# Feed-forward of a hybrid recurrent decoder step: PSUM banks for the main sums, 2 to 3, and for lifted weights, 3 to 2

## The chip, the cores and the metric

The kernel runs on one core of a Trainium2 chip. The metric is the device time of one execution in microseconds (us). Matrix products run on TensorE (PE in the profile; its weight loads are PEld), elementwise work on VectorE (DVE), ScalarE (ACT) and GpSimd (POOL), and SyncE (SP) issues most of the loads. PSUM has 8 banks of 512 fp32 values in each of its 128 partitions; products end there.

## The reference, cut to what matters

One inference step over 512 prompt tokens and 64 sample tokens (576 columns here), width 1024, two layers. Each layer has a SwiGLU feed-forward before its mixer and one behind it, so there are four of them, all with the same shapes (hidden width 2816):

```
def swiglu(x, w_in, w_out):
    a, b = jnp.split(x @ w_in, 2, axis=-1)
    return (jax.nn.silu(a) * b) @ w_out
...
        x = x + 0.5 * swiglu(rmsnorm(x, norm_ffn1[i]), ffn1_w_in[i], ffn1_w_out[i])
...
        x = x + 0.5 * swiglu(rmsnorm(x, norm_ffn2[i]), ffn2_w_in[i], ffn2_w_out[i])
```

## The kernel before, in words

Every product of two fp32 matrices is made of three matmuls of a shorter float type: each operand is split into a high part (a rounded copy) and a low part (what the rounding left), and high x high, low x high and high x low are added up in PSUM.

The greater part of each feed-forward is a list of 30 **units** (`ffn_units`). Units 0 to 2, 7 to 12, 17 to 22 and 27 to 29 are "in" units (one hidden tile of 128 each: its columns of `w_in`), units 3 to 6, 13 to 16 and 23 to 26 are "out" units (two output tiles of x each, over one third of the first 18 hidden tiles). A unit multiplies with a scheme of seven products on blocks of half size, numbered q = 1 to 7, instead of eight; for that the weights are added and subtracted in pairs first (on POOL, `weight_sum`, L2454), and so are the inputs. An "in" product is 12 matmuls of 288 columns, an "out" product 9, all issued at L944 in `pair_product`.

The order of the products is written out by hand (`PE_ORDER`, L87). In step c of the list TensorE issues (c,1), (c-1,7), (c,5), (c,6), (c-1,4), (c-1,3), (c,2), where (u,q) is product q of unit u; the last two of a unit that ends a third (`closes`: units 1, 11, 21, 29) change places. Every other engine has its own order of the same list, and each is a strict queue.

PSUM in this part of the kernel: products 1, 6, 7 and 4 of a unit add up in one bank, the **main sum** (`WBANK`); 5 and 3 in another (`ZBANK`); 2 in bank 3 (`XBANK`). While the sum grows, other engines take it out between the products: after product 1 (semaphore `out1`: a copy on ACT for an "in" unit, an addition to x on DVE, `add_half`, L1796, for an "out" unit), after 6, after 7, and at the end after 4 (`out4`: `last_of_sums` on DVE, L1824 for an "in" unit, L1796 for an "out" unit). Banks change with the unit's number, so the first product of a unit waits until the unit that last had its bank is done: `first_products`, L958, waits for `out4`; product 5 waits for `out3` of the unit two before; product 6 waits for `out1` of its own unit.

**Lifted weights.** For each of the 7 weight blocks of a unit the high part is made on ACT or POOL (`high`), and ACT also copies the fp32 block into a PSUM bank (`lift`, L1228), from where DVE reads it to make the low part (`low`, L1787, a subtraction that writes `wl` or `ff_more_low`). The lifts have one order, `LIFT_ORDER` (L98), and take the banks of a ring in turn; lift number n waits until `low` has read what lay in its bank.

**Hidden blocks.** The hidden tiles come in pairs; DVE and ACT turn a pair into the blocks that the "out" units multiply with (`hidden_sums`, L1880 to L1886; `blocks_high` on ACT, L1277; `blocks_low` on DVE, L1865; semaphore `hb_low`). The last pair of a third is made while the first "out" unit behind it is already in step: its product 1 waits for the first of four blocks of each pair, 5 for two of them, 6 for all four (`blocks_ready`, L949). In DVE's queue the order around an "out" unit that follows a third is: `third_sum`, `low` (4), `last_of_sums`, the gating, `hidden_sums` of the last pair, `low` (6), `first_sum` and `low` (3) of the unit before, `blocks_low` of the last pair (twice), then `add_half` of the out unit's product 1.

On POOL, `high` (L2430) of a weight block waits until the unit before has used the same buffer on TensorE (`product_done`).

Of the kernel before, what the change touches and what calls it, by code (L numbers as in the profile page):

```python
# [52 lines left out]
def ffn_units(f, n):  # L53

    units = []

    def put(kind, **at):
        units.append(Unit(kind, N_UNITS * f + len(units), n + HEAD + 2 * len(units), **at))

    j = HEAD // 2  # L60
    for part in range(3):
        while j <= PART * (part + 1):
            put("in", j=j)
            j += 1
        for m in range(NB // 2):
            put("out", part=part, m=m)
    while j < NTILE:
        put("in", j=j)
        j += 1
    return units  # L70


N_UNITS = NTILE - HEAD // 2 + 3 * NB // 2


def in_order(steps):


    at = {}
    for c in range(-1, N_UNITS + 1):  # L80
        for back, q in steps:
            if 0 <= c - back < N_UNITS:
                at[c - back, q] = len(at) + 1
    return at
# [13 lines left out]
LIFT_ORDER = in_order(((1, 3), (0, 2), (-1, 1), (0, 7), (-1, 5), (0, 4), (-1, 6)))  # L98
# [3 lines left out]
LIFTED = {at: key for key, at in LIFT_ORDER.items()}  # L102
# [60 lines left out]
def count(name, n):  # L163

    n = n if isinstance(n, Lin) else Lin(n)
    assert n.lowest() >= 0 and (not n.k or n.lowest() > 0 or name in FROM_ONE), name
    return (n + 1 if name in FROM_ONE else n).value()
# [7 lines left out]
def build(nc, d, out):  # L175

    at = [16512]
# [9 lines left out]
    ps = nc.alloc_psum_tensor("ps", [P, 8, 512], F32)  # L187
# [57 lines left out]
    def slot(unit, q, low):  # L245
        first = unit.n % 2
        if q in (1, 5, 6):
            return more[low][:, (1, 5, 6).index(q), :]
        ring = (wh, wl)[low][:, first if q in (2, 7) else 1 - first, :]
        return ring[:, 0:512] if q in (2, 3) else ring[:, 512:1024]  # L250

    WBANK, ZBANK, XBANK = (4, 5), (6, 7), 3

    def lift_slot(w, q):
        return ps[:, LIFT_ORDER[w.v % N_UNITS, q] % 3, :]

    def bank(unit, q):
        b = XBANK if q == 2 else (ZBANK if q in (3, 5) else WBANK)[unit.v % 2]
        return ps[:, b, 0:TH]

    at[0] = free
# [73 lines left out]
    def S(name):  # L335
        if name not in sems:
            sems[name] = nc.alloc_semaphore(name)
        return sems[name]
# [12 lines left out]
    for layer in range(2):  # L351
        for kind in ("ffn", "ab" if layer == 0 else "ret", "ffn", "ple"):
            phases.append(dict(kind=kind, layer=layer, n=n, u=u, norm=norm, j=ffj))
            if kind == "ffn":
                units = ffn_units(ffj // TAIL, n)
# [25 lines left out]
    def past(eng, name, n):  # L381

        if n > 0:
            eng.wait_ge(S(name), n)
# [8 lines left out]
    def lo_ready(eng, w, q):  # L393

        if q in (3, 4):
            eng.wait_ge(S("lo_made"), w.n + (2 if q == 3 else 1))
        else:
            eng.wait_ge(S("w_low"), reached(SPLIT_ORDER, w, q))
# [134 lines left out]
    def _(pe):  # L533
# [50 lines left out]
        def gated_group(ns, n, u, i, pair, previous_norm, following=True):  # L584
# [4 lines left out]
            def scores(lev):  # L589
# [25 lines left out]
                for s in range(ns):  # L615
                    j = lev * ns + s
                    bank = 4 + j % 2
                    if j >= 2:
                        pe.wait_ge(S("picked"), count("picked", G("picked", j - 1)))
                    else:  # L620
                        pe.wait_ge(S("orms"), count("orms", G("orms", 0)))
                    for c in range(CH):
                        t = slice(c * P, (c + 1) * P)
                        last = nc.tensor.matmul(ps[:, bank, t], lhsT=ka[rows[s], t], rhs=qa[rows[s], t],
                                                start=True, stop=True)
                    if ns == 1 and lev <= 3:
                        if j:
                            pe.wait_ge(S("picked"), count("picked", G("picked", j)))
                        last = sample(s)
                    last.then_inc(S("scores"), 1)  # L630
# [301 lines left out]
        def pair_product(w, q, free, reached, ready=None):  # L932


            past(pe, free, reached)
            lo_ready(pe, w, q)
            blocks = xt if w.kind == "in" else None
            for k in range(w.pairs):
                if ready is not None:
                    pe.wait_ge(S(ready[0]), ready[1](k))  # L940
                t = slice(k * P, k * P + P)
                for wt, r in ((0, 0), (0, 1), (1, 0)):
                    rhs = (blocks[r][:, k, BLOCK[q], :] if blocks else hblocks[r][k][:, BLOCK[q], :])
                    last = nc.tensor.matmul(bank(w, q), lhsT=slot(w, q, wt)[:, t], rhs=rhs,  # L944
                                            start=(k == 0 and (wt, r) == (0, 0) and q in (1, 5, 2)),
                                            stop=(k == w.pairs - 1 and (wt, r) == (1, 0)), skip_group_check=True)
            last.then_inc(S("product"), 1)

        def blocks_ready(w, units, t):  # L949

            f = w.v // N_UNITS
            if w is units[0]:
                return "xt_low", lambda k: 2 * KP * f + 2 * k + min(t, 2)
            if w.kind == "out" and w.m == 0:
                return "hb_low", lambda k: 4 * 9 * f + 4 * (PART // 2 * w.part + k) + t
            return None

        def first_products(w, units):  # L958

            pair_product(w, 1, "out4", w.v - 1, blocks_ready(w, units, 1))  # L960

        def second_products(w, units):

# [14 lines left out]
        for ph_ in phases:  # L978
            n, u, norm = Lin(ph_["n"]), Lin(ph_["u"]), ph_["norm"]
            if ph_["kind"] == "ffn":  # L980
                j0, units = ph_["j"], ph_["units"]
# [76 lines left out]
    def _(act):  # L1058
# [129 lines left out]
        def ffn(norm, n, u, j0, units):  # L1188
# [14 lines left out]
            def source(w, q):  # L1203

                if q == 1:
                    half_landed(act, w, "11")
                    return half(w.n, 0)
                if q == 2:
                    half_landed(act, w, "12")
                    return half(w.n, 1)  # L1210
                if q == 4:
                    half_landed(act, w, "2")
                    return half(w.n + 1, 1)
                act.wait_ge(S("sum"), reached(SUM_ORDER, w, {7: 3, 5: 1, 6: 2, 3: 4}[q]))
                return half(w.n + 1, 0) if q == 7 else wsum[:, {5: 0, 6: 1, 3: 2}[q], :]

            def lift(w, q):

                c = slice(0, w.pairs * P)
                src = source(w, q)  # L1220
                at = LIFT_ORDER[w.v % N_UNITS, q]
                k, q_before = LIFTED[at - 3]
                lo_ready(act, units[k], q_before)
                if at <= 6:
                    for b in range(2):
                        act.wait_ge(S(f"taken{(u + b).mod(2)}"),
                                    count(f"taken{(u + b).mod(2)}", (u + (HEAD + b)).div(2)))
                nc.scalar.activation(lift_slot(w, q)[:, c], src[:, c], ACT.Copy)\  # L1228
                    .then_inc(S("hi_made" if q in (3, 4) else "lifted"), 1)
# [11 lines left out]
            def snapshot(w, dst, q, free, reached):  # L1241

                past(act, free, reached)
                product_done(act, w, q)
                nc.scalar.activation(dst, bank(w, q), ACT.Copy).then_inc(S(f"out{q}"), 1)
# [39 lines left out]
            w = units[0]  # L1285
# [19 lines left out]
            for c in range(N_UNITS + 1):  # L1305
# [8 lines left out]
                if old:  # L1314
                    lift(old, 3)
# [7 lines left out]
                if new:  # L1323
                    high(new, 2)
                    lift(new, 2)
                if ahead:
                    high(ahead, 1)
                    lift(ahead, 1)
# [217 lines left out]
    def _(dve):  # L1546
# [191 lines left out]
        def ffn(norm, n, u, j0, units):  # L1738
# [33 lines left out]
            def low(w, q):  # L1772

                c = slice(0, w.pairs * P)
                if q in (1, 2):
                    dve.wait_ge(S("act_high"), reached(ACT_HIGH_ORDER, w, q))
                else:
                    dve.wait_ge(S("pool_high"), reached(POOL_HIGH_ORDER, w, q))
                if w is units[0] and q in (1, 5, 6):
                    src = {1: half(w.n, 0), 5: wsum[:, 0, :], 6: wsum[:, 1, :]}[q]  # L1780
                else:
                    src = lift_slot(w, q)
                    if q in (3, 4):
                        dve.wait_ge(S("hi_made"), w.n + (2 if q == 3 else 1))
                    else:
                        dve.wait_ge(S("lifted"), reached(SPLIT_ORDER, w, q) - 3 * (f + 1))
                nc.vector.tensor_tensor(slot(w, q, 1)[:, c], src[:, c], slot(w, q, 0)[:, c], ALU.subtract)\  # L1787
                    .then_inc(S("lo_made" if q in (3, 4) else "w_low"), 1)
# [980 lines left out]
```

## Time and profile before

| | us |
|---|---|
| median of 3 runs | 3002.8 (2998.47 to 3004.94) |
| the profiled execution, its own time | 2996.45 |
| its span, first to last instruction | 2994.8 |
| outside the span | 1.65 |
| TensorE busy in the span | 2715.7 (91%) |
| VectorE busy | 1975.1 (66%) |
| ScalarE busy | 1253.6 (42%) |
| GpSimd busy | 1434.6 (48%) |

The unit lists of the four feed-forwards begin at 73.9, 937.5, 1430.3 and 2546.2 us of the span. A busy TensorE is matmuls in the pipe, not matmuls at full speed: each row carries the granted clock beside it where it matters (1.00 is 2.4 GHz, 0.50 is 1.2 GHz). In a timeline the bracket behind an instruction is the idle time of its engine just before it and what ended that time.

### The profile page before, as it was taken

To read this page: it belongs to the slowest core of one execution; us is meant where nothing else is said; L and a number is where in the kernel's file an instruction comes from. 1 tells how busy PE (TensorE), PEld (TensorE's weight loads), DVE (VectorE), ACT (ScalarE), POOL (GpSimd) and SP (SyncE) were. 2 spreads that over 40 slices of the span, in tenths; PEclk is the share of its full clock that TensorE was granted. 3 is DMA by queue.
4 is the path that set the end of the run, shared out by engine and by line. 5 is a ranking of instruction groups with operands and counts; after the bars stand their busy time and mean duration, and the time that the engine had idled before them with its cause. 6 is when DMAs were issued, how large, how long until landed. Compare 5 with 4: busy or idle time off the path is not lost. (4 is left out here: it accounts for less than half of the span.)

```text
span 2994.8 us, 51957 instructions
## 1 busy us (share of the span) xinstructions
PE 2715.7 (91%) x19034; PEld 2566.9 (86%) x19034; DVE 1975.1 (66%) x2876; ACT 1253.6 (42%) x2267; POOL 1434.6 (48%) x1469
## 2 busy tenths in 40 slices
PE   7899999899888999998899999889897979899997
PEld 7899998788788999998899998687786869899996
DVE  7887767765658788648877854352625247877865
ACT  4565553222134556534565552122122224565552
POOL 4677734443227777515677742130303116677731
PEclk9999999999989999999999999989998989999998
DMA  3223221121122222321223223412323222222221
GB/s 121 82 81 97 88 96 65 56 72 53 37 63 69 94 87 81 98 91 57 75 93 91 82 85 105 155 61 106 111 84 138 78 99 74 79 84 94 88 87 60
DMA packets 109059, 255.92 MB, mean 85 GB/s; under 512 B 12496, under 2 KB 37216, under 8 KB 108816
## 3 DMA queue, kind: packets, MB, share of 16 engines
q1 hardware_dynamic: 96192, 206.73, 21.5%
q0 software_dynamic: 12624, 45.98, 4.2%
q8 instruction: 150, 2.46, 0.3%
q14 instruction: 93, 0.76, 0.1%
HBM read 227.88 MB, written 24.77 MB: 84 GB/s over the span
## 5 line engine op out<-in xcount | busy, mean ns | idle before, releaser
L1787 DVE TENSOR_TENSOR wl<-ps,wh 128x512 fp32r<-128x512 f32 (+1 forms) x480 | 304.2, 634 | 172.5 <-ACT ps L1228 100.9
L1552 DVE TENSOR_TENSOR wl<-raw,wh 128x1024 fp32r<-128x1024 f32 x169 | 224.7, 1330 | 219.8 <-ACT wh L1066 218.9
L944 PE MATMUL ps<-ff_x_high,wh 128*128 128x288 f32 x1152 | 345.9, 300 | 0.0
L944 PE MATMUL ps<-ff_x_low,wh 128*128 128x288 f32 x1152 | 345.9, 300 | 0.0
L944 PE MATMUL ps<-ff_x_high,wl 128*128 128x288 f32 x1152 | 344.5, 299 | 0.0
L562 PE MATMUL ps<-xh,wh 128*128 128x288 f32 x1248 | 301.4, 324 | 32.6 <-DVE xl L1574 19.0
L1228 ACT ACTIVATE ps<-ff_w_sums 128x512 f32<-128x512 f32 (+1 forms) x352 | 190.7, 551 | 309.4 <-POOL ff_w_sums L2454 309.2
L1066 ACT ACTIVATE wh<-raw 128x1024 fp32r<-128x1024 f32 x169 | 178.0, 1054 | 319.6 <-PE ps L540 191.4
L944 PE MATMUL ps<-ff_x_high,ff_more_high 128*128 128x288 f32 x864 | 257.4, 298 | 30.0 <-DVE ff_hidden L1824 26.1
L562 PEld LDWEIGHTS ps<-xh,wh 128*128 128x128 f32 x1248 | 207.7, 197 | 80.8 <-issue 59.3
L562 PE MATMUL ps<-xh,wl 128*128 128x288 f32 x1248 | 274.8, 303 | 0.0
L562 PE MATMUL ps<-xl,wh 128*128 128x288 f32 x1248 | 273.9, 302 | 0.0
L1787 DVE TENSOR_TENSOR ff_more_low<-ps,ff_more_high 128x512 fp32r<-128x512 f32 (+1 forms) x348 | 218.9, 629 | 71.9 <-POOL ff_more_high L2430 47.9
L1228 ACT ACTIVATE ps<-raw 128x512 f32<-128x512 f32 (+1 forms) x476 | 256.6, 545 | 11.5 <-DVE ff_more_low L1787 11.5
L944 PE MATMUL ps<-ff_x_low,ff_more_high 128*128 128x288 f32 x864 | 255.8, 296 | 0.0
L944 PE MATMUL ps<-ff_x_high,ff_more_low 128*128 128x288 f32 x864 | 255.6, 296 | 0.0
L2430 POOL CAST wh<-raw 128x512 fp32r<-128x512 f32 (+1 forms) x240 | 149.0, 621 | 191.2 <-PE ps L944 185.8
L2454 POOL TENSOR_TENSOR ff_w_sums<-raw,ff_w_sums 128x512 f32<-128x512 f32 (+1 forms) x120 | 157.0, 1308 | 162.1 <-issue 129.8
L944 PEld LDWEIGHTS ps<-ff_x_high,wh 128*128 128x128 f32 x1152 | 223.3, 194 | 0.0
L944 PEld LDWEIGHTS ps<-ff_x_low,wh 128*128 128x128 f32 x1152 | 223.2, 194 | 0.0
L944 PEld LDWEIGHTS ps<-ff_x_high,wl 128*128 128x128 f32 x1152 | 222.6, 193 | 0.0
L562 PEld LDWEIGHTS ps<-xl,wh 128*128 128x128 f32 x1248 | 208.0, 196 | 0.0
(339 smaller groups left out, 7549.9 us busy)
## 6 DMA issues: line engine op xcount, KB each, us to landing
raw<-in_w SPq DMA_DIRECT2D x169, 512.0 KB, 3.4
raw<-in_w SPq DMA_DIRECT2D x288, 256.0 KB, 2.6
raw<-in_w SPq DMA_DIRECT2D x192, 192.0 KB, 2.3
rS<-in_s_ret POOLq DMA_DIRECT2D x32, 512.0 KB, 6.2
out_ret_s<-rS POOLq DMA_DIRECT2D x32, 512.0 KB, 3.7
x<-in_xT SPq DMA_DIRECT2D x8, 288.0 KB, 5.9
out_yT<-x SPq DMA_DIRECT2D x8, 288.0 KB, 2.2
S<-in_s_hgrn POOLq DMA_DIRECT2D x4, 512.0 KB, 3.6
```

The costliest lines, as they stand in the source:

```text
L562: last = nc.tensor.matmul(ps[:, 2 * s + a, 0:TH], lhsT=wt[:, slot, w], rhs=rhs(r, k)[:, a * TH:(a + 1) * TH], start=(k == 0 and j == 0), s ...
L944: last = nc.tensor.matmul(bank(w, q), lhsT=slot(w, q, wt)[:, t], rhs=rhs, start=(k == 0 and (wt, r) == (0, 0) and q in (1, 5, 2)), stop=(k ...
L1066: nc.scalar.activation(wh[:, n.mod(2), :], raw[:, r, :], ACT.Copy).then_inc(S("hi_made"), 1)
L1228: nc.scalar.activation(lift_slot(w, q)[:, c], src[:, c], ACT.Copy)\
L1552: nc.vector.tensor_tensor(wl[:, n.mod(2), :], raw[:, n.mod(NRAW), :], wh[:, n.mod(2), :], ALU.subtract)\
L1787: nc.vector.tensor_tensor(slot(w, q, 1)[:, c], src[:, c], slot(w, q, 0)[:, c], ALU.subtract)\
L2430: nc.gpsimd.tensor_copy(slot(w, q, 0)[:, c], src[:, c]).then_inc(S("pool_high"), 1)
L2454: nc.gpsimd.tensor_tensor(out_[:, c], in0[:, c], in1[:, c], op).then_inc(S("sum"), 1)
```

## The change

The main sums get three banks in turn (4, 5, 2) in place of two, and the first product of a unit waits for the unit three before it in place of two before. Bank 2 is taken from the ring of lifted weights: it has two banks (0, 1) in place of three, and a lift waits for the `low` two before it in the order in place of three before. No instruction is added or removed, and none changes its place in its engine's queue.

```diff
-    WBANK, ZBANK, XBANK = (4, 5), (6, 7), 3
+    WBANK, ZBANK, XBANK = (4, 5, 2), (6, 7), 3
 
     def lift_slot(w, q):
-        return ps[:, LIFT_ORDER[w.v % N_UNITS, q] % 3, :]
+        return ps[:, LIFT_ORDER[w.v % N_UNITS, q] % 2, :]
 
     def bank(unit, q):
-        b = XBANK if q == 2 else (ZBANK if q in (3, 5) else WBANK)[unit.v % 2]
+        b = XBANK if q == 2 else ZBANK[unit.v % 2] if q in (3, 5) else WBANK[(unit.v + 1) % 3]
         return ps[:, b, 0:TH]
...
         def first_products(w, units):
 
-            pair_product(w, 1, "out4", w.v - 1, blocks_ready(w, units, 1))
+            pair_product(w, 1, "out4", w.v - 2, blocks_ready(w, units, 1))
...
                 at = LIFT_ORDER[w.v % N_UNITS, q]
-                k, q_before = LIFTED[at - 3]
+                k, q_before = LIFTED[at - 2]
                 lo_ready(act, units[k], q_before)
```

## Rows read from the trace of the kernel before

**Rows 1.** Waits of TensorE, whole span: total us, times, longest us.

```profile
PE ps L944 <- DVE ff_hidden L1824: 47.6, 32, 5.4
PE ps L944 <- DVE x L1796: 33.0, 10, 3.9
```

**Rows 2.** Timeline of TensorE, first feed-forward, stops: start us, us, instruction.

```profile
94.38 0.40 PE L944 MATMUL ps<-ff_x_high,ff_more_high 128*128 128x288 f32 x1 [2.71 <-DVE ff_hidden L1824]
...
111.18 0.85 PE L944 MATMUL ps<-ff_blocks_a,ff_more_high 128*128 128x288 f32 x2 [5.40 <-DVE ff_hidden L1824]
...
182.37 0.40 PE L944 MATMUL ps<-ff_x_high,ff_more_high 128*128 128x288 f32 x1 [1.46 <-DVE ff_hidden L1824]
...
194.13 0.40 PE L944 MATMUL ps<-ff_x_high,ff_more_high 128*128 128x288 f32 x1 [0.37 <-DVE ff_hidden L1824]
...
216.96 0.53 PE L944 MATMUL ps<-ff_blocks_a,ff_more_high 128*128 128x288 f32 x2 [0.31 <-DVE ff_hidden L1824]
...
225.10 0.53 PE L944 MATMUL ps<-ff_blocks_a,ff_more_high 128*128 128x288 f32 x2 [3.90 <-DVE x L1796]
```

**Rows 3.** Timeline of VectorE and TensorE, first feed-forward, steps 3 and 4.

```profile
106.23 0.77 DVE L1865 TENSOR_TENSOR ff_blocks_b<-ff_hidden,ff_blocks_b 128x288 fp32r<-128x288 f32 x1
...
115.54 1.88 DVE L1865 TENSOR_TENSOR ff_blocks_b<-ff_hidden_sums,ff_blocks_b 128x864 fp32r<-128x864 f32 x1
117.34 0.44 DVE L1796 SCALAR_TENSOR_TENSOR x<-ps,x 128x288 f32<-128x288 f32 x1
...
117.84 0.53 PE L944 MATMUL ps<-ff_blocks_a,ff_more_high 128*128 128x288 f32 x2
```

**Rows 4.** All waits of VectorE between 99 and 117.7 us.

```profile
DVE wl L1787 <- ACT ps L1228: 1.8, 2, 1.1
```

**Rows 5.** Windows (columns: PE, PEld, DVE, ACT, POOL busy; PEclk, DMA): first, third feed-forward.

```profile
111.18:117.84 6.66, 6.66 (x30) 6.43 (x30) 5.91 (x11) 4.50 (x9) 2.53 (x3) 0.59 0.19 60
...
1468.29:1474.96 6.67, 5.75 (x30) 5.51 (x31) 5.92 (x11) 4.50 (x9) 2.75 (x3) 0.74 0.18 59
```

**Rows 6.** Windows of 9 us behind a restart of TensorE, same columns.

```profile
117.84:126.84 9.00, 9.00 (x69) 9.00 (x69) 7.67 (x18) 4.35 (x10) 6.46 (x10) 1.00 0.29 87
...
1950.84:1959.84 9.00, 9.00 (x45) 8.43 (x46) 6.83 (x6) 2.09 (x4) 5.57 (x4) 0.69 0.16 58
...
225.10:234.10 9.00, 9.00 (x56) 9.00 (x57) 6.16 (x14) 3.39 (x8) 4.93 (x8) 0.81 0.26 70
...
1582.31:1591.31 9.00, 9.00 (x49) 9.00 (x50) 5.48 (x12) 2.80 (x7) 4.82 (x7) 0.70 0.22 66
```

**Rows 7.** Timeline of TensorE: the stop ahead of the second of those windows.

```profile
1950.84 0.82 PE L884 MATMUL ps<-sqsum,ones 128*128 128x288 f32 x1 [7.82 <-POOL sqsum L2545]
```

**Rows 8.** Timeline of VectorE: `low` (2,2), first and third feed-forward.

```profile
98.20 0.69 DVE L1787 TENSOR_TENSOR wl<-ps,wh 128x512 fp32r<-128x512 f32 x1 [0.78 <-ACT ps L1228]
...
1456.45 0.69 DVE L1787 TENSOR_TENSOR wl<-ps,wh 128x512 fp32r<-128x512 f32 x1 [2.17 <-ACT ps L1228]
```

**Rows 9.** All waits of VectorE between 182 and 224.9 us.

```profile
DVE wl L1787 <- ACT ps L1228: 2.7, 4, 0.8
DVE wl L1787 <- POOL wh L2430: 2.0, 2, 1.6
```

**Rows 10.** Timeline of GpSimd and VectorE, first feed-forward, steps 12 and 13.

```profile
215.20 0.62 POOL L2430 CAST wh<-raw 128x512 fp32r<-128x512 f32 x1 [2.43 <-PE ps L944]
...
215.85 0.69 DVE L1787 TENSOR_TENSOR wl<-ps,wh 128x512 fp32r<-128x512 f32 x1 [1.56 <-POOL wh L2430]
```

**Rows 11.** Timeline of ScalarE and VectorE: lift (2,5), `low` (2,1), `low` (2,5).

```profile
89.49 0.59 ACT L1228 ACTIVATE ps<-ff_w_sums 128x512 f32<-128x512 f32 x1
...
92.09 0.68 DVE L1787 TENSOR_TENSOR ff_more_low<-ps,ff_more_high 128x512 fp32r<-128x512 f32 x1
...
93.28 0.68 DVE L1787 TENSOR_TENSOR ff_more_low<-ps,ff_more_high 128x512 fp32r<-128x512 f32 x1
```

## The prediction

> **What bounds the kernel now.** I read the table of waits first. Inside the unit lists TensorE stops for two reasons only: 47.6 us in 32 stops for L1824, the last sum of an "in" unit, and 33.0 us in 10 stops for L1796, an addition to x [rows 1]. The first is the wait that the change loosens: a unit's first product wants the bank of the unit two before. The second looks like the same wait and is not. The timeline of the first feed-forward [rows 2] shows the stops in order: 2.71 (unit 2), 5.40 (unit 3, the first "out" unit), then 1.46, 0.37 and 0.31 ahead of units 10, 11 and 13, and 3.90 at 225.10. That last one is not at the first product of a unit: it is product 6 of unit 13, 8.1 us later, and what it waits for is `out1` of its own unit, the addition of product 1 to x. A third bank for main sums does not touch it. Units 20, 21, 23 repeat the pattern, so a feed-forward has 8 stops for L1824, and 4 x 8 = 32.
>
> So the question is what else holds TensorE where the stops are. Both stretches with stops lie around the end of a third, where VectorE makes the blocks of the last hidden pair on top of its sums and low parts, and VectorE is late there by its own queue. Between 99 and 117.7 us it waits 1.8 us in all, for ScalarE and never for TensorE [rows 4]. TensorE's product (3,6) needs the addition that VectorE ends at 117.34 + 0.44 = 117.78, and starts at 117.84 [rows 3]. That it is bound by VectorE the windows show best: from the start of (3,1) to the start of (3,6) it takes 6.66 us in the first feed-forward and 6.67 in the third, though TensorE ran at a granted clock of 0.59 in the one and of 0.74, with 0.9 us of idle, in the other [rows 5].
>
> **The change part by part.** Nothing is added, removed or moved in a queue, so no operation, load or issue has a new price. What changes is two waits: `out4` gets a whole step more room, the lifts lose one bank of room. No DMA hangs on either: the loads of weights wait for low parts and sums of units that keep their place.
>
> (a) Units 2 and 3, the first two stops of each feed-forward (8.11 us in the first). Without them the first block that (3,1) still waits for is written by 106.23 + 0.77 = 107.0 [rows 3]; from there 3 matmuls of (3,1), 12 of (2,7) and 9 of (3,5), at 9.00 / 69 = 0.13 us each [rows 6], bring TensorE to (3,6) at 107.0 + 3.1 = 110.1. There it waits for the addition at 117.78 as before: one stop of 7.7 us in place of the two. VectorE's chain up to that addition has no wait for TensorE that could shrink [rows 4], so the gain is 0 (bounds: 0, and 5.40 if the chain came along). In the third feed-forward there is one: `low` (2,2) waited 2.17 us there and 0.78 in the first [rows 8], because the late (2,1) held up ScalarE's copy ahead of it. I take 1.2 us of gain, once (bounds 0 and 1.4).
>
> (b) The clock. Before, TensorE leaves (3,6) at full clock: 69 matmuls in 9 us, granted clock 1.00; it had gone slow after the stop of 5.40 and came back while it would have waited anyway. With one stop of 7.7 us right ahead of (3,6) it restarts slow. The nearest row is the restart after a stop of 7.82 us [rows 7]: clock 0.69 over the next 9 us, which is 9 x 0.31 = 2.8 us of lost work; after a stop of 3.90 it is 0.81, so 1.7 [rows 6]. I take the middle, 2.2, four times: 8.8 us slower (bounds 0 and 4 x 2.8 = 11.2). The Trainium skill, "TensorE: Matmul & The Clock Gate", section "What's actually happening", puts it as "the default state is throttled, and activity releases the throttle". The trace agrees, with 0.69 behind the longest stop; by that rule, gathering two stops into a longer one is a loss by itself.
>
> (c) Units 10, 11, 13 and 20, 21, 23: stops of 1.46 + 0.37 + 0.31 = 2.14 us, eight times. TensorE comes earlier to (13,6) and waits there for VectorE. What survives is what VectorE's chain gains. From 182 to 224.9 us it waits 2.7 us for ScalarE, which itself follows VectorE's sums, and 2.0 us in two waits for GpSimd [rows 9]; the larger, 1.56 us, is `low` (12,4) behind a cast that GpSimd could not start before TensorE's product (11,4) had ended [rows 10]. Only these 2.0 come back when TensorE is earlier. I take half, 0.95, since the lift of the same block on ScalarE ends soon after: 8 x 0.95 = 7.6 us faster (bounds 0 and 2.0 each). The stop at (13,6) grows from 3.90 to 3.90 + 2.14 - 0.95, about 5.1. After the 3.90 the clock over 9 us was 0.81 in one case and 0.70 in another [rows 6], so the longer stop costs between 0 and 9 x 0.11 = 1.0 more; I take 0.3, near the smaller as the stop is nearer to 3.90 than to 7.82: 2.4 us slower.
>
> (d) The ring of two. A lift now waits for the `low` two before. The worst place that I found is lift (2,5): it started at 89.49, ahead of the time, and would have to wait for `low` (2,1) to end, 92.09 + 0.68 = 92.77; with 0.59 for itself it is done at 93.36, while `low` (2,5) started at 93.28 [rows 11]. With the signals between, some 0.3 us late, inside VectorE's late chain: 4 x 0.3 = 1.2 us slower. Elsewhere the early lifts lie far ahead of their use and the wait costs nothing; if that cover is gone, a lift is late by up to the whole 92.77 - 89.49 = 3.3 us. Behind a waiting lift stand ScalarE's snapshots and SiLUs, which VectorE's sums release anyway. Bounds: 0 and 4 x 3.3 = 13.2.
>
> Sum: -1.2 (a) + 8.8 (b) - 7.6 + 2.4 (c) + 1.2 (d) = +3.6 us. On the profiled execution's own 2996.45 that is 3000; the median of the runs, 3002.8, lies 6.35 above that execution, and by it the forecast is **3006 us**. About 0.2%, 6 us, is what a measurement can tell from no change, so this is no change with a lean to slower.
>
> **The rivals.** *The stops simply go.* The stops for L1824 vanish and nothing late stands behind them: 3002.8 - 47.6 = 2955. The Trainium skill, "Perfetto Trace Analysis", section "Identifying Performance Opportunities", says that the same gap repeating on the engine that should be saturated can mean too few buffers; by that rule the third bank is the cure. The trace does not bear it out: (3,6) keeps its time whatever TensorE did [rows 5]. *VectorE comes along.* The wait for GpSimd goes whole and no restart is slower than now: 8 x 2.0 = 16 us faster, 2987. For it: 2.0 us in [rows 9] hang on TensorE. Against it: ScalarE's lift. *The clock decides.* The place is the restart at (3,6), and at (13,6) and (23,6): where a stop has grown, the slow clock lasts as in the worst rows, 4 x 2.8 + 8 x 1.0 = 19.2 us, and VectorE gains nothing: 3022, slower. It decides if the stops at (3,6) are 7 us and more. *The ring of two holds VectorE back*: 13.2 us, 3016; it shows as longer waits of L1787 for L1228 (1.8 and 2.7 us in the two stretches now [rows 4, 9]). That the change doesn't do what it says has no room: the counts of `out4` and the banks agree.
>
> **How the numbers follow.** The forecast gets 0.50, and its own range is 2997 to 3012: 0.42 of it within 0.2%, 0.06 above, 0.02 below. The stops go: 0.06. VectorE comes along: 0.13. The clock decides: 0.21. The ring: 0.10, of which 0.02 within. Faster 0.02 + 0.06 + 0.13 = 0.21; same 0.42 + 0.02 = 0.44; slower 0.06 + 0.21 + 0.08 = 0.35. The range reaches from just below VectorE coming along to just under the clock's full price, 2984 to 3020; it leaves out the 0.06 at 2955 and the ends.
>
> **What would show it.** In the profile of the changed kernel no stop of L944 for L1824 is left; the stops for L1796 rise from 33.0 us in 10 to some 4 x 7.7 + 8 x 5.1 = 72 us in 12; (3,6) starts within 0.5 us of where it did against the list's begin, save in the third feed-forward; the 9 us behind it read a clock below 0.9. If (3,6) starts 3 us or more earlier, (a) is wrong and with it the forecast; if the clock behind it is 1.00, (b) is; if L1787's waits for L1228 double, (d) is too small.

## The result and the profile after

The changed kernel takes 3003.2 us, the median of 20 runs (2999.7 to 3009.2), against 2998.0 us (2991.7 to 3004.9) in 20 runs of the kernel before on the same chip: a ratio of 1.0018, with a 95% interval of 1.0012 to 1.0025. That is 5 us slower: less than the 0.2% (6 us) below which the prediction speaks of no change, though the interval keeps clear of 1. The profiled execution took 3008.81 us (span 3006.9, mean granted clock 0.956, before 0.961); it lies 5.6 us above its median and the one of before 1.6 us below its own, so the two traces differ by 12.4 us where the medians differ by 5.2. The unit lists now begin at 72.7, 943.0, 1439.6 and 2556.2 us.

TensorE's waits in the changed kernel (total us, times, longest us), to be read against [rows 1]:

```profile
PE ps L944 <- DVE x L1796: 61.8, 12, 7.3
...
PE ps L944 <- issue: 11.5, 7, 2.8
...
PE ps L944 <- DVE ff_more_low L1787: 5.8, 4, 2.0
...
PE ps L944 <- DVE ff_c L1815: 3.7, 8, 0.5
PE ps L944 <- DVE ff_a L1834: 2.5, 8, 0.4
```

All 32 stops for L1824 are gone, 47.6 us of them. The stops for an addition to x have grown by 28.8 us, and there are 12 of them, one at product 6 of each first output unit of a third. The rest came back in small stops: the last three rows are new, and the second had

```profile
PE ps L944 <- issue: 3.9, 4, 1.0
```

before. With a last stop of 0.2 us, all that TensorE waits in the unit lists (L944) is 84.5 us before and 85.5 after: the bank moved its idle time and took none of it away. The timeline of TensorE, first feed-forward, shows where ([rows 2] before; start us, us, instruction, idle before it):

```profile
105.76 0.57 PE L944 MATMUL ps<-ff_blocks_a,ff_more_high 128*128 128x288 f32 x1 [2.79 <-issue]
...
116.95 0.61 PE L944 MATMUL ps<-ff_blocks_a,ff_more_high 128*128 128x288 f32 x1 [5.45 <-DVE x L1796]
...
125.24 0.43 PE L944 MATMUL ps<-ff_blocks_a,ff_more_high 128*128 128x288 f32 x2
...
226.04 0.61 PE L944 MATMUL ps<-ff_blocks_a,ff_more_high 128*128 128x288 f32 x1 [4.72 <-DVE x L1796]
```

Product (3,1) starts at 105.76, 33.0 us into the list in place of 37.2 (111.18 before). Product (3,6) starts 44.2 us into it in place of 43.9, so the 4.2 us won at (3,1) are waited away again: 5.45 us at one product. The line at 125.24 is (4,1); the kernel before had it at

```profile
123.51 0.43 PE L944 MATMUL ps<-ff_blocks_a,ff_more_high 128*128 128x288 f32 x2
```

From (3,6) to (4,1) are 5.67 us there (117.84 to 123.51) and 8.29 us here, with the same work. The four windows of 9 us behind (3,6) say why (columns: busy us and instructions of PE, PEld, DVE, ACT, POOL; the granted clock; DMA share and GB/s):

```profile
116.95:125.95 9.00, 9.00 (x48) 9.00 (x49) 5.39 (x12) 3.19 (x8) 4.81 (x7) 0.67 0.20 66
987.36:996.36 9.00, 9.00 (x48) 9.00 (x49) 5.45 (x12) 3.11 (x8) 4.52 (x7) 0.67 0.23 66
1484.39:1493.39 9.00, 9.00 (x55) 9.00 (x56) 6.09 (x14) 3.80 (x9) 4.84 (x7) 0.79 0.26 67
2600.53:2609.53 9.00, 9.00 (x55) 9.00 (x56) 6.07 (x14) 3.78 (x9) 4.86 (x7) 0.79 0.23 67
```

Before, the clock behind this product was 1.00 in all four feed-forwards [rows 6 for the first]. Now 0.33, 0.33, 0.21 and 0.21 of 9 us are missing: 9.7 us of full clock. The same windows behind product 6 of units 13 and 23, after:

```profile
226.04:235.04 9.00, 9.00 (x47) 9.00 (x48) 5.38 (x12) 3.13 (x7) 4.82 (x7) 0.67 0.21 66
335.17:344.17 9.00, 9.00 (x47) 9.00 (x48) 5.33 (x12) 3.08 (x7) 4.82 (x7) 0.66 0.21 67
1096.46:1105.46 9.00, 9.00 (x47) 9.00 (x48) 5.39 (x12) 3.14 (x7) 4.82 (x7) 0.67 0.23 66
1205.60:1214.60 9.00, 9.00 (x47) 9.00 (x48) 5.34 (x12) 3.10 (x7) 4.82 (x7) 0.66 0.22 66
1592.60:1601.60 9.00, 9.00 (x51) 9.00 (x52) 5.61 (x13) 3.59 (x8) 4.87 (x7) 0.73 0.23 66
1701.20:1710.20 9.00, 9.00 (x49) 9.00 (x50) 5.48 (x12) 3.39 (x8) 4.82 (x7) 0.70 0.23 66
2708.68:2717.68 9.00, 9.00 (x51) 9.00 (x52) 5.59 (x13) 3.59 (x8) 4.86 (x7) 0.73 0.24 66
2817.32:2826.32 9.00, 9.00 (x49) 9.00 (x50) 5.48 (x12) 3.37 (x8) 4.82 (x7) 0.70 0.25 67
```

The eight windows of before are the two in [rows 6], three more of 0.81 in the first two feed-forwards, and these three:

```profile
1691.99:1700.99 9.00, 9.00 (x51) 9.00 (x52) 5.55 (x13) 2.97 (x7) 4.85 (x7) 0.72 0.21 66
2697.59:2706.59 9.00, 8.99 (x58) 9.00 (x59) 6.48 (x15) 3.62 (x9) 5.16 (x8) 0.84 0.28 78
2806.14:2815.14 9.00, 9.00 (x56) 9.00 (x57) 6.27 (x14) 3.39 (x8) 4.93 (x8) 0.81 0.25 72
```

What is missing to 1.00 sums to 1.69 windows before and 2.48 after, 15.2 and 22.3 us: 7.1 us more. Over all 12 restarts it is 15.2 us of full clock before and 32.0 after. The time lost is a little less, as the table below shows.

What the change gives stands in VectorE's waits over the whole span, before (first two lines, one kernel) and after (the next fence):

```profile
DVE wl L1787 <- ACT ps L1228: 100.9, 116, 2.2
DVE wl L1787 <- POOL wh L2430: 67.2, 141, 1.6
```

```profile
DVE wl L1787 <- ACT ps L1228: 109.8, 124, 2.1
DVE wl L1787 <- POOL wh L2430: 49.3, 119, 0.7
```

The waits for GpSimd's casts fell by 17.9 us, and 8.9 us of that came back as waits for ScalarE's lifts. In the first feed-forward (4,1) to (13,6) takes 100.80 us in place of 101.59: 0.79 us won.

The starts of the products give the whole account in time. Each row is a sum over the four feed-forwards, in us:

| stretch | before | after | more |
|---|---|---|---|
| begin of the list to (3,6) | 176.6 | 177.6 | 1.0 |
| (3,6) to (4,1), behind the first restart | 22.7 | 31.3 | 8.6 |
| (4,1) to (13,6) and (14,1) to (23,6) | 812.8 | 806.4 | -6.4 |
| (13,6) to (14,1) and (23,6) to (24,1), behind the other two | 58.9 | 65.3 | 6.4 |
| (24,1) to the end of the list | 248.7 | 248.7 | 0.0 |
| the four lists | 1319.7 | 1329.4 | 9.7 |

The spans of the two profiled executions differ by 12.1 us; the other 2.4 us lie outside the lists. That rest of the span is not steady: over all the profiled executions of this document it lies between 1666.4 and 1678.5 us. So the lists are compared by traces and whole kernels by medians.

### The profile page after: what moved, and what is told of

It is laid out like the page before. It is cut to its first block and busy times, and to the rows that moved or that the text cites. A ratio compares the mean times of both kernels' runs of the same rounds, so it can differ in the third digit from the quotient of the medians.

```text
span 3006.9 us, 51956 instructions
## 1 busy us (share of the span) xinstructions
PE 2724.1 (91%) x19034; PEld 2577.1 (86%) x19034; DVE 1975.8 (66%) x2876; ACT 1264.4 (42%) x2267; POOL 1434.4 (48%) x1469
## 5 line engine op out<-in xcount | busy, mean ns | idle before, releaser
L1787 DVE TENSOR_TENSOR wl<-ps,wh 128x512 fp32r<-128x512 f32 (+1 forms) x480 | 304.0, 633 | 164.3 <-ACT ps L1228 109.8
L944 PE MATMUL ps<-ff_x_high,wh 128*128 128x288 f32 x1152 | 349.6, 304 | 3.7 <-DVE ff_c L1815 3.7
L944 PE MATMUL ps<-ff_x_low,wh 128*128 128x288 f32 x1152 | 348.8, 303 | 0.0
L944 PE MATMUL ps<-ff_x_high,wl 128*128 128x288 f32 x1152 | 347.8, 302 | 0.0
L1228 ACT ACTIVATE ps<-ff_w_sums 128x512 f32<-128x512 f32 (+1 forms) x352 | 190.9, 551 | 300.6 <-POOL ff_w_sums L2454 225.3
L1228 ACT ACTIVATE ps<-raw 128x512 f32<-128x512 f32 (+1 forms) x476 | 261.8, 550 | 43.8 <-DVE wl L1787 37.1
L944 PE MATMUL ps<-ff_x_high,ff_more_high 128*128 128x288 f32 x864 | 255.7, 296 | 12.1 <-DVE ff_more_low L1787 5.8
L1787 DVE TENSOR_TENSOR ff_more_low<-ps,ff_more_high 128x512 fp32r<-128x512 f32 (+1 forms) x348 | 219.0, 629 | 72.4 <-POOL ff_more_high L2430 47.0
L944 PE MATMUL ps<-ff_x_low,ff_more_high 128*128 128x288 f32 x864 | 255.0, 295 | 0.0
L944 PE MATMUL ps<-ff_x_high,ff_more_low 128*128 128x288 f32 x864 | 254.7, 295 | 0.0
L944 PEld LDWEIGHTS ps<-ff_x_high,wh 128*128 128x128 f32 x1152 | 226.6, 197 | 5.5 <-DVE ff_c L1815 5.5
L944 PEld LDWEIGHTS ps<-ff_x_low,wh 128*128 128x128 f32 x1152 | 225.9, 196 | 0.0
L944 PEld LDWEIGHTS ps<-ff_x_high,wl 128*128 128x128 f32 x1152 | 225.4, 196 | 0.0
```

## The experiments

Ratios are to the kernel before, timed on the same chip beside it, with their 95% interval. Line numbers move a little where an edit adds lines.

### The ring of two alone

```diff
-        return ps[:, LIFT_ORDER[w.v % N_UNITS, q] % 3, :]
+        return ps[:, LIFT_ORDER[w.v % N_UNITS, q] % 2, :]
...
-                k, q_before = LIFTED[at - 3]
+                k, q_before = LIFTED[at - 2]
```

> The kernel before with the ring of lifted weights cut to two banks and nothing else; the third bank for main sums is not there. My theory (the clock takes back what the third bank gives, the ring is a small term): +0.3 us per feed-forward, so about +1 us, ratio to the kernel before 1.000 to 1.001, with the stops for L1824 and for L1796 within 2 us of the kernel before (47.6 and 33.0 us). The rival (the shorter ring holds VectorE back and is the whole loss of the change): +5 us or more, ratio 1.0017 or above, and the waits of L1787 for L1228 clearly longer than before.

Measured: 2995.5 us against 2998.9, ratio 0.9998 (0.9988 to 1.0009). TensorE's waits in it:

```profile
PE ps L944 <- DVE ff_hidden L1824: 46.7, 32, 4.1
PE ps L944 <- DVE x L1796: 33.5, 12, 3.9
```

The stops are those of the kernel before, and the waits of L1787 for L1228 are 102.7 us in place of 100.9 (`wl`) and 24.3 in place of 23.3 (`ff_more_low`). The place that the prediction named is there: `low` (2,5) now waits for its lift,

```profile
92.66 0.69 DVE L1787 TENSOR_TENSOR ff_more_low<-ps,ff_more_high 128x512 fp32r<-128x512 f32 x1 [0.20 <-ACT ps L1228]
```

and starts 19.6 us into the list in place of 19.3 [rows 11]. Product (3,6) comes 0.4 to 0.6 us later in each feed-forward, 2.1 us in all, which the interval of 3 us to either side can't show. The shorter ring has a price, but it isn't the loss.

### The looser wait at units 2 and 3 only, and everywhere but there

Both keep the three banks and the ring of two; a first product that may not use the new room waits for `out4` of the unit two before, as it did before the change.

```diff
-            pair_product(w, 1, "out4", w.v - 2, ...)
+            pair_product(w, 1, "out4", w.v - (2 if w in units[2:4] else 1), ...)   # units 2 and 3 only
+            pair_product(w, 1, "out4", w.v - (1 if w in units[2:4] else 2), ...)   # everywhere else
```

> The changed kernel with the looser wait only at units 2 and 3 of each feed-forward; every other unit's first product waits for `out4` of the unit just before it, as it did before the change. Theory (the loss lies at the restart behind product 6 of unit 3, and the later thirds give and take about the same): unit 4 starts 1.7 to 3.1 us later than in the kernel before in each feed-forward, as in the changed kernel, and nothing is won or lost later: about 9 us slower than the kernel before, ratio 1.003. Rival (the loss is that of the later thirds): within 2 us of the kernel before.

> The other half: the changed kernel with the stricter wait at units 2 and 3, so that the looser one is left to the later units alone. Theory: the stop of 5 us at unit 3 comes back ahead of its time, product 6 of unit 3 restarts at full clock, and what is left is 8 times a gain of VectorE of 0.8 us less 0.8 us of clock: within 3 us of the kernel before, ratio 0.999 to 1.001, so 5 us or more below the changed kernel. Rival: as slow as the changed kernel, 3003.

Measured: units 2 and 3 only, 3006.3 us against 2996.8, ratio 1.0023 (1.0012 to 1.0035); everywhere else, 2997.1, ratio 1.0000 (0.9990 to 1.0009). The window behind (3,6), first in the kernel with units 2 and 3 only, then in the other:

```profile
117.64:126.64 9.00, 9.00 (x56) 9.00 (x57) 6.23 (x14) 3.96 (x9) 4.91 (x8) 0.81 0.25 68
```

```profile
117.23:126.23 9.00, 9.00 (x68) 9.00 (x69) 7.67 (x18) 4.96 (x11) 6.46 (x10) 1.00 0.31 87
```

And in the second kernel, the stop at (3,1), now back:

```profile
110.57 0.40 PE L944 MATMUL ps<-ff_blocks_a,ff_more_high 128*128 128x288 f32 x1 [4.13 <-DVE ff_hidden L1824]
```

So the loss is made at units 2 and 3, about 7 us, by a stop that has moved from (3,1), where the clock came back while TensorE would have waited anyway, to (3,6), where the slow clock has nothing to hide behind. At the later thirds gain and loss cancel within 3 us. In the trace of the second kernel VectorE's 6.4 us are won as in the changed kernel, and the eight stops at units 13 and 23 are as long, 4.7 us. But the stretches behind them take only 2.6 us more than before, not 6.4; the worst and the best of the eight windows read

```profile
1198.42:1207.42 9.00, 9.00 (x49) 9.00 (x50) 5.48 (x12) 3.37 (x8) 4.81 (x7) 0.70 0.25 66
...
2699.11:2708.11 9.00, 9.00 (x57) 9.00 (x58) 6.35 (x15) 4.06 (x10) 5.01 (x8) 0.82 0.26 70
```

### VectorE's chain made longer

On the changed kernel; one subtraction is done twice (the first result is overwritten with the same values).

```diff
                         blocks_low(j, 1, 0)
+                        ...
+                        nc.vector.tensor_tensor(hblocks[1][k][:, 4:7, :], hsum[:, 1:4, :],
+                                                hblocks[0][k][:, 4:7, :], ALU.subtract).then_inc(S("twice"), 1)
+                        ...
+                        dve.wait_ge(S("twice"), TWICE[0])
                         blocks_low(j, 1, 1)
```

> The changed kernel, with one subtraction of VectorE done twice at the end of each third of the hidden units: the low parts of the last pair's three late blocks (L1865, 128x864, 1.2 to 1.9 us), 12 places. It lies ahead of the addition to x that product 6 of the first output unit waits for. Theory (a): that product starts when VectorE's chain ends, so it starts later by 1.3 to 2.0 us at each of the 12 places, and the kernel takes 12 x that longer, 16 to 24 us more than the changed kernel, 3019 to 3027. Rival: TensorE's own work or the weights set the start, and the stop is only where slack is spent; then the kernel is longer by under 6 us.

Measured: 3011.0 us against 2998.9, ratio 1.0051 (1.0035 to 1.0068). Against the changed kernel's 3003.2 that is 8 us (some 5 to either side, by the interval), outside both expectations. VectorE, first feed-forward:

```profile
114.79 1.87 DVE L1940 TENSOR_TENSOR ff_blocks_b<-ff_hidden_sums,ff_blocks_b 128x864 fp32r<-128x864 f32 x1
116.70 1.24 DVE L1866 TENSOR_TENSOR ff_blocks_b<-ff_hidden_sums,ff_blocks_b 128x864 fp32r<-128x864 f32 x1
117.86 0.45 DVE L1797 SCALAR_TENSOR_TENSOR x<-ps,x 128x288 f32<-128x288 f32 x1
```

The addition starts at 117.86, 45.00 us into the list; in the changed kernel it was 116.45, 43.73 us into it: 1.27 us later, and TensorE's (3,6) with it (118.36, after a stop of 6.27). That much of the theory holds: VectorE's chain sets the start. It moved by about 1.27 us at eleven places and by 0.83 at (3,6) of the third feed-forward, 14.8 us in all. But the windows behind the 12 restarts, of which four are these,

```profile
118.36:127.36 9.00, 9.00 (x47) 9.00 (x48) 5.29 (x12) 3.04 (x7) 4.35 (x7) 0.66 0.22 66
228.85:237.85 9.00, 9.00 (x51) 9.00 (x52) 5.57 (x13) 3.58 (x8) 4.37 (x7) 0.73 0.24 67
...
1487.04:1496.04 9.00, 9.00 (x58) 9.00 (x59) 6.51 (x15) 4.23 (x10) 4.71 (x8) 0.84 0.26 77
1596.13:1605.13 9.00, 9.00 (x57) 9.00 (x58) 6.46 (x15) 4.15 (x10) 4.65 (x8) 0.83 0.25 77
```

read, but for the first, better than the changed kernel's 0.67, 0.67, 0.79 and 0.73. Over all 12, 2.85 windows are missing in place of 3.56: 6.4 us less, all of it at units 13 and 23 (by the starts of the products 5.6 us less). 14.8 - 5.6 = 9.2, which is what the four lists grew by, against the 8 measured. Longer stops cost less clock here; why is in the last section.

### TensorE kept busy in the stop

```diff
+            if w.kind == "out" and w.m == 0:
+                pe.wait_ge(S("out2"), w.v)
+                for _ in range(6):
+                    nc.tensor.matmul(ps[:, XBANK, 0:TH], lhsT=ones[:, :], rhs=rinv[:, 0:TH],
+                                     start=True, stop=True)
             pair_product(w, 6, "out1", w.v + 1, blocks_ready(w, units, 4))
```

> The changed kernel, with six float32 matmuls of a 128x288 tile issued into the bank of product 2 right ahead of each product 6 that stops for an addition to x (12 places); their result is used by nothing. They lie inside the stop, so they keep TensorE busy for a part of it and delay nothing unless a stop is shorter than they take. If the restart at half clock is what costs (theory: about 12 x 2 to 3 us of lost work stand behind these stops in the changed kernel, of which the kernel before paid the part behind units 13 and 23), the kernel is faster than the changed one by 10 to 30 us and the 9 us behind the stops read a granted clock of 0.9 or more. If the clock costs nothing there (rival: VectorE sets the time behind the stops too, so slow TensorE is covered), the clock rises and the time stays within 3 us of the changed kernel, 3003. A third outcome, the same clock as before, would say that this much work is too little to keep it up, and leaves the question open.

Measured: 2973.0 us against 2998.9, ratio 0.9921 (0.9904 to 0.9938), 30 us below the changed kernel. TensorE in the first feed-forward, and the windows behind (3,6) and (13,6):

```profile
113.60 3.18 PE L968 MATMUL ps<-rinv,ones 128*128 128x288 f32 x12 [0.78 <-DVE ff_a L1811]
117.83 0.40 PE L944 MATMUL ps<-ff_blocks_a,ff_more_high 128*128 128x288 f32 x1 [1.05 <-DVE x L1801]
```

```profile
117.83:126.83 9.00, 9.00 (x68) 9.00 (x69) 7.68 (x18) 4.97 (x11) 6.45 (x10) 1.00 0.33 89
224.29:233.29 9.00, 9.00 (x68) 9.00 (x69) 7.67 (x18) 4.97 (x11) 6.45 (x10) 1.00 0.31 89
```

(3,6) starts 44.2 us into its list (which begins at 73.6), as without the extra work; only the clock is another. All 12 windows read 1.00, and the four lists take 1301.2 us, 28.2 less than in the changed kernel; the 12 stretches behind the restarts alone are 28.5 us shorter. That is what the slow restarts cost, a little less than the 32.0 us of clock read above, and close to the 30 us measured.

The same on the kernel before, at all 12 places, and then at the 8 of units 13 and 23 only (` and w.part` added to the condition):

> The kernel before with the same six float32 matmuls ahead of product 6 at the same 12 places (the result is used by nothing). There the 4 restarts at unit 3 were at full clock already, and the extra matmuls may even delay them where the stop is short; the 8 at units 13 and 23 read 0.81 and 0.70 over 9 us, so 1.7 to 2.7 us each are to be had: 14 to 22 us faster than the kernel before, 2977 to 2984. Theory: with the clock held up in both, the third bank keeps what it gives VectorE, 8 x 0.8 us and a little in the third feed-forward, so the changed kernel with these matmuls (2973) stays 5 to 11 us below this one. Rival (the third bank gives nothing even then): this kernel within 3 us of 2973.

> The kernel before with the six extra matmuls (their result is used by nothing) only ahead of product 6 of units 13 and 23, 8 places; unit 3, where they had delayed product 6 by 1.6 to 2.6 us in the run with all 12 places, is left alone. From that run's clock at the 8 places, about 1.5 us each: 12 us faster than the kernel before, 2983 to 2987 (and 1.6 to 2.6 us four times, or about 9 us, below the run with all 12 would be 2979). Theory: the clock held up in both, the third bank is worth VectorE's 8 x 0.8 us, so the changed kernel with these matmuls (2973) is 5 to 12 us below this one. Rival (with the clock held up the third bank gives nothing): 2970 to 2976.

Measured: 12 places, 2988.4 us, ratio 0.9967 (0.9954 to 0.9980), a miss; 8 places, 2982.6, ratio 0.9948 (0.9933 to 0.9964), just below what was expected. With 12, the extra matmuls run from 117.09 to 120.16 in the first feed-forward, just when (3,6) could have started: there is no stop left to put them in, and the four (3,6) start 8.7 us later in all. With 8, the 9 us behind (13,6) read

```profile
225.10:234.10 9.00, 9.00 (x70) 9.00 (x69) 7.67 (x18) 4.36 (x10) 6.44 (x10) 1.00 0.33 89
```

and the 15 us won are the slow restarts of before: 13.6 us by the starts of the products. With the clock held up in both, the kernel with the third bank is the faster one, by 9.7 us in the medians (2982.62 and 2972.96). They come from two chips, and the intervals of the two ratios overlap a little. The lists agree in sign and not in size: 1306.2 and 1301.2 us, 6.4 won by VectorE less 1.2 ahead of (3,6). The gain is there, 5 us of it by the traces, and the clock hid it.

### Real work in the stop

A version in which TensorE issues products 4 and 3 of the unit before, ready by then, ahead of product 6, and VectorE does what they and product 6 wait for ahead of the last pair's blocks. The same sums in another order:

```diff
             pair_product(w, 5, "out3", w.v - 1, blocks_ready(w, units, 2))
+            if w.kind == "out" and w.m == 0:
+                old = units[units.index(w) - 1]
+                pair_product(old, 4, "out7", old.v + 1)
+                pair_product(old, 3, "out5", old.v + 1)
             pair_product(w, 6, "out1", w.v + 1, blocks_ready(w, units, 4))
...
                 if closes(older):
+                    second_sum(old)
+                    add_half(new, 1, 0, 1)
                     for j, first, second in steps:
                         blocks_low(j, 1, 0)
                         blocks_low(j, 1, 1)
```

(The places where these calls stood, and `PE_ORDER`, are changed to match.) It was run with the banks of after and of before:

> The changed kernel with the order around the 12 long stops changed: TensorE issues products 4 and 3 of the unit before ahead of product 6 of the first output unit, and VectorE does that unit's second sum and the addition of product 1 ahead of the two block subtractions of the last pair (0.75 and 1.2 to 1.9 us). By the theory (stops of 4.7 to 7.3 us behind VectorE's chain, TensorE otherwise the bound) each stop loses the 2 to 3 us of work that is put into it and the later restart is less slow: 12 x 2 to 3.5 us, 24 to 42 us faster than the changed kernel, 2961 to 2979. Rival: VectorE's queue is the bound through the whole stretch, so TensorE only waits at another product and the time stays within 5 us of 3003.

> The kernel before with the changed order of the products and of VectorE's work around the 12 long stops, and two banks for main sums as before. Theory: the long stops are filled in part here too, but the 32 stops for L1824 (46.7 to 47.6 us in all) stay, and what they cost is now on the path, since VectorE's chain ahead of product 6 has been made shorter: slower than the same order with the third bank (2963) by 8 x 1.5 to 2.1 us and more at the first units, so 2975 to 2990. Rival: the third bank is worth nothing with this order either, 2960 to 2966.

Measured: three banks, 2962.8 us, ratio 0.9884 (0.9863 to 0.9904); two banks, 2968.4, ratio 0.9895 (0.9878 to 0.9911), outside both expectations and near the rival's. The order is worth 28 to 40 us. The third bank on top of it is worth nothing that shows: the medians differ by 5.6 us, which these intervals do not settle, and the four lists take 1288.1 and 1288.5 us. The reason is the old one over again. In unit 13's step TensorE now stops for VectorE's second sum, with three banks and then with two:

```profile
218.96 0.40 PE L949 MATMUL ps<-ff_x_high,wh 128*128 128x288 f32 x1 [2.28 <-DVE ff_c L1824]
```

```profile
221.10 0.40 PE L949 MATMUL ps<-ff_x_high,wh 128*128 128x288 f32 x1 [1.44 <-DVE ff_c L1824]
```

and the 9 us behind read 0.81 and 1.00. So that sum was moved as well, ahead of two operations of VectorE that it doesn't need:

```diff
+                if closes(older):
+                    second_sum(old)
                 if old:
                     first_sum(old)
                     low(old, 3)
                 if closes(older):
-                    second_sum(old)
                     add_half(new, 1, 0, 1)
```

> The changed kernel with the new order around the 12 stops and one step more: at these places VectorE does the second sum of the unit before (0.45 us) ahead of its first sum and of the low part of product 3's weights, which in the run with the new order alone came first, with 0.72 to 0.78 us of waiting for ScalarE's lift and 0.69 us of work. The stops of 2.3 to 4.5 us for that second sum should each shrink by 1.38 us, and the half-clock stretches behind them go in part: 12 x 1.4 to 3 us below 2963, so 2927 to 2946. Rival: the same wait comes back at the next product (product 6 and the last pair's blocks, which now have 1.4 to 3.0 us to spare), and less than 8 us is won.

> The same order as the last kernel (TensorE's two products and VectorE's second sum and addition moved ahead), but with the banks and the waits of the kernel before: two banks for main sums, three for lifted weights. Theory (the third bank pays as soon as VectorE's chain no longer sets the end of each third): the 32 stops for L1824, 47 to 49 us in all, stay here and their cost is not covered by a later stop, so 12 to 22 us slower than the same order with the third bank (2943): 2955 to 2965. Rival (the third bank is worth no more with this order than it was with the first one, where the two were within 6 us): 2938 to 2949.

Measured: three banks, 2943.1 us, ratio 0.9815 (0.9798 to 0.9831); two banks, 2963.1, ratio 0.9884 (0.9867 to 0.9900). TensorE's largest waits in the unit lists, three banks, then two:

```profile
PE ps L949 <- DVE ff_c L1824: 14.3, 20, 3.1
```

```profile
PE ps L949 <- DVE ff_hidden L1833: 56.9, 44, 5.4
```

Here the third bank is worth 20 us (the lists take 1268.6 and 1289.1), and the version with it beats the kernel before by 54 us and the changed one by 60. With two banks the wait for the main sum (L1833, the old L1824) is what remains; with three it is gone, and what stands behind it now is small: 14.3 us in 20 stops for VectorE's second sum.

## Why the prediction was right, and where its terms were off

The forecast was 3006, 3.6 us above the median of three runs that it started from, no change with a lean to slower. Measured were 3003.2, 5.2 us above the 2998.0 of 20 runs: slower, and by less than 0.2%. Step by step:

- **(a), the two stops become one: right in place, off in size.** (3,6) starts 0.3, 0.4, 0.1 and 0.2 us later into the list than before, all inside the 0.5 us named. The stop measures 5.45, 5.79, 7.33 and 5.42 us in place of 7.7. (3,1) started where the step had it, 33.0 us into the list, but behind a stop of 2.79 us, and TensorE took 5.74 us and not 3.1 to the next stop, at a clock of 0.70 and not at full clock. So the stops for L1796 came to 61.8 us and not 72. The 1.2 us of the third feed-forward didn't show; (3,6) is not earlier there.
- **(b), the slow restart: right, 8.6 us by the starts (9.7 by the windows) against 8.8**, and shown by three runs: units 2 and 3 only (+7), everywhere else (0), TensorE kept busy (-30, at all 12 places). The rule quoted there, by which activity releases the throttle (the Trainium skill, "TensorE: Matmul & The Clock Gate", section "What's actually happening"), agrees: 3.18 us of activity in the stop turned 0.67 into 1.00. The step's reading that a longer stop costs more is wrong; see the last section. It put the price between the rows behind a stop of 7.82 us (0.69) and one of 3.90 (0.81), and that the four came out near its middle is luck: 0.67 stood behind 5.45 us and 0.79 behind 7.33.
- **(c), VectorE: right.** Half of GpSimd's wait was to come back and half to turn into waits for the lift: 17.9 us went and 8.9 came back. The 0.95 us per third is 0.79. **The clock at units 13 and 23 is the mis-sized term: 2.4 us predicted, 6.4 in this execution by the starts (7.1 by the windows).** The stop itself grew less than predicted, to 4.7 us and not 5.1. The step took the stop's length as the measure, between two rows of 3.90 us with 0.81 and 0.70, and put the new one near the better; here it came out at 0.66 to 0.73. But the run with the looser wait everywhere but at units 2 and 3, with stops of the same 4.7 us, read 0.70 to 0.82 and 2.6 us by the starts, close to the 2.4. So the term differs from execution to execution, and which size the median execution has stays open.
- **(d), the ring: right.** 1.2 us was the term, by a `low` (2,5) that starts 0.3 us later. It does, and (3,6) comes 1.0 us later in all in the changed kernel and 2.1 in the run with the ring alone, too little for the medians (0.9998).

By the trace the terms are 8.6 - 6.4 + 6.4 + 1.0 = 9.7 us in the lists (the 1.0 are the four small delays of (3,6)), against the 3.6 of the sum; the medians have 5.2. So the forecast owes some of its closeness to the medians: measured against its own pair of executions, the sum was 6 us short, 4.0 of them in that one term.

Of the rivals, "The stops simply go" is out: they moved, 84.5 us to 85.5. The rule beside it (the Trainium skill, "Perfetto Trace Analysis", section "Identifying Performance Opportunities": the same gap repeating can mean too few buffers) does not hold for the kernel as it stood, 5 us slower with the buffer, and does hold after VectorE's order was changed, 20 us faster with it. "VectorE comes along" is out in size: 6.4 us came and not 16, and the restarts became slower. "The clock decides" had the right place; its 19.2 us is more than the 15.0 by the starts (16.8 by the windows), and VectorE's gain, which it denied, was there. The ring with its 13.2 us is refuted by its own run.

## What to carry to other kernels

Before a buffer is added for a wait, look for what the stalled engine would wait for next, and whether that work depends on the engine at all: if another engine's own queue sets it, the stop only moves. Where it moves to matters: a stop with slack behind it hides the clock's return, and one on the path pays for it. Shorten the late chain first (here by moving two small operations ahead of two large ones, and ready work into the stop), and measure the buffer again: it went from 5 us lost to 20 us won.

## What the runs showed of the hardware

**A longer stop may cost less clock.** In the changed kernel, the stop of 5.45 us and the one of 7.33 us, each with the slow stretch behind it:

```profile
111.50:116.95 5.45, 0.00 (x1) 0.00 (x1) 4.74 (x8) 3.39 (x7) 2.74 (x3) 0.91 0.14 49
116.95:122.80 5.85, 5.85 (x24) 5.85 (x25) 3.39 (x8) 1.48 (x3) 1.73 (x3) 0.50 0.22 67
...
1477.06:1484.39 7.33, 0.01 (x2) 0.00 (x1) 6.58 (x13) 4.08 (x8) 2.74 (x3) 0.79 0.17 54
1484.39:1488.15 3.76, 3.76 (x15) 3.76 (x16) 2.99 (x7) 1.49 (x3) 1.42 (x2) 0.50 0.37 87
```

The clock fell to its lower level, 1.2 GHz, while TensorE stood still, in the first case shortly before the restart (0.91 over the stop) and in the second well before (0.79); 5.85 and 3.76 us of work then ran at 0.50. What counts is how much of the slow stretch is left when work begins, and the stop's length alone does not give it: across these runs stops of 5.45, 6.27, 7.33 and 8.23 us were followed by 0.67, 0.66, 0.79 and 0.84, and in one trace stops of 5.45 and 5.42 us by 0.67 and 0.79. That is what gave back 5.6 of the 14.8 us in the run with the longer chain. A microsecond at 0.50 is not quite half lost: 24 matmuls in 5.85 us are 0.24 us each, against 0.13 at full clock [rows 6].

**Work without a use can pay.** Six matmuls of 3.18 us in all, put into a stop that was there anyway, won 30 us over 12 places; where there was no stop to hide them, at (3,6) of the kernel before, they cost 8.7 us over four. And with the stops filled by useful work the kernel went lower than that, to 2943.
